# A planner for the weight slots of a two-pass decoder layer: resident w_down blocks, serpentine order, lookahead eviction

## The reference, cut to what matters

```python
h = rmsnorm(x, g_pre_mix)
p = h @ w_in                      # 1024 x 6144: xv | B | C | u | gate_conv | gate_pool
ya = (B * causal_dwconv3(C * xv)) @ w_out_conv
yb = pool_scale * groupwise_linear(trailing_mean_w(u) - u)   # w in (2, 4, 8, 16)
merged = sigmoid(gate_conv) * ya + sigmoid(gate_pool) * yb
x = x + rmsnorm(merged @ w_o, g_post_mix)
f = square(relu(rmsnorm(x, g_pre_mlp) @ w_up)) @ w_down      # 1024 x 4096, 4096 x 1024
x = x + rmsnorm(f, g_post_mlp)
```

## Time and profile before

| | |
|---|---|
| median of 3 runs | 1152.27 us (1150.86 to 1153.66) |
| the profiled execution | 1154.85 us |
| its span on the slowest core (core 0) | 1153.8 us |
| spans of the 8 cores | 1133.2 to 1153.8 us |
| mean granted TensorE clock of the cores | 0.952 to 0.961 |
| DMA traffic of core 0 | 136.50 MB |
| weight loads of the plan | 96, of which 48 from wd_bf |
| stages on core 0: w_up of pass 1, w_down of pass 1 | 322 to 431.5 us, 431.5 to 570.2 us |
| w_up of pass 2, w_down of pass 2 | 892 to 1015 us, 1015 to 1153 us |

### The profile page before, as it was taken

How to read it: one execution, slowest core, us unless ns; L and a number is a source line. 1 busy time by engine, 2 the same in 40 slices (tenths; PEclk the granted TensorE clock), 3 DMA queues, 4 the chain that set the end, 5 groups by cost and what they waited for, 6 DMA issues and landing times.

```text
span 1153.8 us, 15517 instructions; the slowest of 8 cores (1133.2 to 1153.8 us)
## 1 busy us (share of the span) xinstructions
PE 1028.5 (89%) x5289; PEld 487.0 (42%) x5289; DVE 477.2 (41%) x838; ACT 340.3 (29%) x643; POOL 173.6 (15%) x183
## 2 busy tenths in 40 slices
PE   3799689899699999888879999988976999999996
PEld 1344334344344444433335555534532555544442
DVE  4555334573533441413136655456444344412022
ACT  2322212225723333312112233322365333301011
POOL 6010002333400000000200002134043000000100
PEclk9799889899899999988979999989998999999999
DMA  9999926939353228763990743361585232136651
GB/s 213 132 135 137 131 39 81 139 33 146 60 91 74 74 74 297 242 219 112 224 167 1 111 58 53 48 100 21 114 181 104 43 74 74 74 146 237 218 201 55
DMA packets 82913, 136.50 MB, mean 118 GB/s; under 512 B 15107, under 2 KB 70467, under 8 KB 76676
## 3 DMA queue, kind: packets, MB, share of 16 engines
q0 software_dynamic: 75552, 109.58, 51.4%
q1 hardware_dynamic: 7168, 25.89, 6.7%
q10 hardware_dynamic: 116, 0.03, 0.0%
HBM read 185.11 MB, written 18.49 MB: 176 GB/s over the span
## 4 chain that ended last, share of the span: by engine, by line
PE 71%; DMA 12%; DVE 7%; issue 4%; ACT 4%; POOL 1%; DVEq 0%; ACTq 0%; SPq 0%; POOLq 0%
PE PS L121 70%; DMA WS<-w_in 4%; DMA TM<-x_p 4%; DMA WS<-w_out_conv 4%; ACT TM L138 3%; DVE TM L151 2%; DVE TM L141 2%; DVE AR L141 1%; PE PS L125 1%; DVE AR L151 1%; POOL AR L141 1%; DVE STAT L517 1%; ACT STAT L138 1%; ACT AR L138 0%; DVEq L206 0%
## 5 line engine op out<-in xcount | busy, mean ns | idle before, releaser
L121 PE MATMUL PS<-AR,WS 128*128 128x512 bf16 (+1 forms) x3520 | 682.5, 356 | 54.4 <-DVE AR L141 20.8
L121 PEld LDWEIGHTS PS<-AR,WS 128*128 128x128 bf16 x3520 | 320.3, 100 | 406.5 <-issue 91.5
L121 PE MATMUL PS<-WS,AR 128*128 128x512 bf16 x1360 | 308.4, 387 | 17.4 <-DVE TM L151 8.4
L138 ACT ACTIVATE TM<-PS 128x512 f32<-128x512 f32 (+3 forms) x270 | 158.3, 597 | 444.7 <-PE PS L121 425.9
L121 PEld LDWEIGHTS PS<-WS,AR 128*128 128x128 bf16 x1360 | 133.5, 99 | 183.1 <-issue 35.2
L141 DVE TENSOR_TENSOR AR<-TM 128x512 bf16<-128x512 f32 (+1 forms) x184 | 111.8, 622 | 164.1 <-ACT TM L138 160.8
L517 DVE RECIPROCAL STAT<-STAT 128x1 f32<-128x1 f32 x68 | 10.9, 160 | 216.6 <-ACT STAT L138 216.4
L112 POOL DMA_DIRECT2D WS<-wd_bf x48 | 25.5, 532 | 367.0 <-PE PS L121 291.6
L141 DVE TENSOR_TENSOR TM<-PS,TM 128x512 f32<-128x512 f32 (+1 forms) x56 | 35.5, 634 | 106.1 <-PE PS L121 104.3
L151 DVE SCALAR_TENSOR_TENSOR TM<-TM,CS 128x512 f32<-128x512 f32 (+1 forms) x80 | 53.7, 672 | 39.1 <-ACT TM L138 34.9
L141 POOL TENSOR_TENSOR TM<-TM 128x526 f32<-128x526 f32 (+3 forms) x36 | 42.6, 1182 | 133.1 <-ACT TM L138 69.6
(11 more groups left out here) (64 smaller groups left out, 359.4 us busy)
## 6 DMA issues: line engine op xcount, KB each, us to landing
WS<-wd_bf POOLq DMA_DIRECT2D x48, 1024.0 KB, 6.3
WS<-w_in POOLq DMA_DIRECT2D x21, 1024.0 KB, 27.2
WS<-w_up POOLq DMA_DIRECT2D x16, 1024.0 KB, 13.9
wd_bf<-w_down POOLq DMA_DIRECT2D x8, 1024.0 KB, 29.6
TM<-x_p SPq DMA_DIRECT2D x16, 512.0 KB, 6.9
y_p<-AR SPq DMA_DIRECT2D x16, 512.0 KB, 7.0
AR<-x_p SPq DMA_DIRECT2D x8, 512.0 KB, 10.9
WS<-w_out_conv POOLq DMA_DIRECT2D x4, 1024.0 KB, 14.4
```

The costliest lines, as they stand in the source:

```text
L121: return self.add("pe", lambda e: e.matmul(out, lhsT, rhs, start=start, stop=stop), reads=[lhsT, rhs], writes=[out], signal=sig, name="mm")
L138: return self.add("act", lambda e: e.activation(out, in_, func, **kw), reads=rd, writes=wr, name=name)
```

## The change

The slots are planned ahead. For each entry in order the new code looks whether its block is still in a slot; if so, nothing is loaded. If not, it takes, among the slots that its own group does not use, the one whose content is needed again latest within the entries e+1 to e+63 (not at all counts as latest), and of equals the one used longest ago. `free_after` holds the group that last used the slot. A load is issued when its own group is asked for, or earlier, at the first group g for which `free_after < g`; the loads still go out in the order of the entries. And every second token-tile group of the w_down stage runs through its eight blocks in reversed order (7 to 0), so that its first blocks are the last ones of the group before; `start` and `stop` of the accumulation follow the order. In pass 1 that is the second of three groups, in pass 2 too; the plan and the stage use the same function.

```diff
--- before.py
+++ after.py
@@ -353,6 +353,10 @@
             slot_ctr[0] += 1
             return s
 
+        def s5_order(gi_):
+            od = [(nh, kg) for nh in range(2) for kg in range(4)]
+            return od if gi_ % 2 == 0 else od[::-1]
+
         plan = []
         for ps_i in range(npass):
             nt_ = NPP // 128 + (1 if (with_sample and ps_i == npass - 1) else 0)
@@ -364,16 +368,49 @@
             plan.append([(w_o, 0, 0), (w_o, 0, 512)])
             for blk in range(DFF // 512):
                 plan.append([(w_up, 0, blk * 512)])
-            for a in range(0, nt_, 3):
-                for nh in range(2):
-                    for kg in range(4):
-                        plan.append([(w_down, kg * 1024, nh * 512)])
+            for gi_, a in enumerate(range(0, nt_, 3)):
+                for (nh, kg) in s5_order(gi_):
+                    plan.append([(w_down, kg * 1024, nh * 512)])
         entries = [e for g in plan for e in g]
         gfirst = []
+        gof = []
         acc_ = 0
-        for g in plan:
+        for gi_, g in enumerate(plan):
             gfirst.append(acc_)
             acc_ += len(g)
+            gof += [gi_] * len(g)
+        keyof = [(id(W_), r_, c_) for (W_, r_, c_) in entries]
+        slot_of, need_load, free_after = [], [], []
+        content = [None] * NSLOT
+        last_use = [-1] * NSLOT
+        for e, k_ in enumerate(keyof):
+            if k_ in content and e >= 3:
+                sl_ = content.index(k_)
+                slot_of.append(sl_)
+                need_load.append(False)
+                free_after.append(-1)
+            else:
+                same_grp = [slot_of[e2] for e2 in range(gfirst[gof[e]], e)]
+                best, best_key = None, None
+                for sl_ in range(NSLOT):
+                    if sl_ in same_grp:
+                        continue
+                    if content[sl_] is None:
+                        nu = 10 ** 9
+                    else:
+                        nu = 10 ** 9
+                        for e2 in range(e + 1, min(len(keyof), e + 64)):
+                            if keyof[e2] == content[sl_]:
+                                nu = e2
+                                break
+                    cand = (nu, -last_use[sl_])
+                    if best_key is None or cand > best_key:
+                        best, best_key = sl_, cand
+                slot_of.append(best)
+                need_load.append(True)
+                free_after.append(gof[last_use[best]] if last_use[best] >= 0 else -1)
+                content[best] = k_
+            last_use[slot_of[e]] = e
         wstate = {"g": 0, "issued": 0, "conv": 0}
         conv_ops = []
 
@@ -381,9 +418,9 @@
             def __init__(self, e, split):
                 self.split = split
                 if split:
-                    self.v = _view(WS, (e % NSLOT) * 8192, BF16, [4, KC, 128])
+                    self.v = _view(WS, slot_of[e] * 8192, BF16, [4, KC, 128])
                 else:
-                    self.v = _view(WS, (e % NSLOT) * 8192, BF16, [KC, 512])
+                    self.v = _view(WS, slot_of[e] * 8192, BF16, [KC, 512])
 
             def lhsT(self, k, jj):
                 return self.v[:, jj, k, :] if self.split else self.v[:, k, jj * 128:(jj + 1) * 128]
@@ -414,12 +451,18 @@
                     if c == 7:
                         for op_ in conv_ops:
                             op_.dma = ("wdc", P.dma_cnt["wdc"])
-            while wstate["issued"] < len(entries) and (wstate["issued"] < first + cnt or
-                                                       (wstate["issued"] - NSLOT < first and not (g == 0 and not topup))):
+            while wstate["issued"] < len(entries):
                 e = wstate["issued"]
-                assert e - NSLOT < first
+                own = e < first + cnt
+                ahead_ok = (free_after[e] < g) and not (g == 0 and not topup)
+                if not (own or ahead_ok):
+                    break
+                if own:
+                    assert free_after[e] < g
                 W, r0, c0 = entries[e]
-                if e < 3:
+                if not need_load[e]:
+                    pass
+                elif e < 3:
                     if e == 0:
                         for jj_ in range(4):
                             for e_ in range(3):
@@ -430,10 +473,10 @@
                                       deps=([xload0[min(3, len(xload0) - 1)]] if (jj_ > 0 and xload0) else []))
                 elif W is w_down:
                     src = wd_bf[(r0 // 1024) * 2 + (c0 // 512), :, :].rearrange("p (k c) -> p k c", c=512)
-                    P.dma("pool", wslot_view(e).v, src, "w%d" % (e % NSLOT), name="wload_bf", deps=conv_ops)
+                    P.dma("pool", wslot_view(e).v, src, "w%d" % slot_of[e], name="wload_bf", deps=conv_ops)
                 else:
                     src = W[r0:r0 + KC * 128, c0:c0 + 512].rearrange("(k p) c -> p k c", p=128)
-                    P.dma("pool", wslot_view(e).v, src, "w%d" % (e % NSLOT), name="wload")
+                    P.dma("pool", wslot_view(e).v, src, "w%d" % slot_of[e], name="wload")
                 wstate["issued"] += 1
             return [wslot_view(first + i) for i in range(cnt)]
 
@@ -920,17 +963,19 @@
                 bk = {}
                 for gi_, i in enumerate(G):
                     bk[i] = 2 * gi_
-                for nh in range(2):
-                    for kg in range(4):
-                        wd, = wgroup([(w_down, kg * 1024, nh * 512)])
-                        if unit_i >= 1 and pending_s0:
-                            pending_s0.pop(0)()
-                        unit_i += 1
-                        for i in G:
-                            for kk in range(KC):
-                                P.mm(PS[:, bk[i] + nh, :], actT[:, kg * 8 + kk, i * 128:(i + 1) * 128], wd.full(kk),
-                                     start=(kg == 0 and kk == 0), stop=(kg == 3 and kk == KC - 1),
-                                     signal=((kg == 3 or i == G[-1]) and kk == KC - 1))
+                od_ = s5_order(groups.index(G))
+                for (nh, kg) in od_:
+                    kgs_ = [kg2 for (nh2, kg2) in od_ if nh2 == nh]
+                    first_k, last_k = (kg == kgs_[0]), (kg == kgs_[-1])
+                    wd, = wgroup([(w_down, kg * 1024, nh * 512)])
+                    if unit_i >= 1 and pending_s0:
+                        pending_s0.pop(0)()
+                    unit_i += 1
+                    for i in G:
+                        for kk in range(KC):
+                            P.mm(PS[:, bk[i] + nh, :], actT[:, kg * 8 + kk, i * 128:(i + 1) * 128], wd.full(kk),
+                                 start=(first_k and kk == 0), stop=(last_k and kk == KC - 1),
+                                 signal=((last_k or i == G[-1]) and kk == KC - 1))
                 for i in G:
                     pm = bass.AP(PS, bk[i] * 512, [[4096, 128], [1, D]])
                     ss = stat()
```

## The result

The changed kernel takes 1370.79 us in the median (1365.16 us the fastest), against 1152.85 us before; the ratio is 1.189, with a 95% interval of 1.185 to 1.193. The prediction was 1408, range 1368 to 1450: the direction came out as written, and so did the mechanism in the main; the size was 37 us too large.

A forecast was written before the change was run, and what follows sets the result against it. TensorE, busy 89% of the span, bounds the kernel, so its standstills are paid in full. Lost prefetch, clock ramps and w_down relief sum to 255.9 us: 1154.85 + 255.9 - 2.6 = 1408 us, range 1368 to 1450.

The forecast's parts named there:

- The farthest next use belongs to the slot that was used last: Planner, pass 1: most blocks recur 48 entries later, inside the 63-entry window, so the slot just used is evicted.
- The reason given for lateness: Late groups: loads go out in order, issued only after the previous group's last matmul, so TensorE waits for issue and transfer.
- Groups 39 to 41: Pass 2, before w_up: bursts of late loads add 24.1 us each in groups 39 and 40, 17.8 in group 41.
- The length of a burst: Four loads issued together: the fourth ends near 30 us, 30.6 with 0.6 before it, at 138 GB/s.
- Groups 2 and 3: Pass 1, w_in and w_out_conv: late bursts of four loads plus two clock ramps add 7.9 and 18.4 us.
- Groups 6 to 12: Pass 1 w_up blocks: seven stalls of 8.7 us plus a 2.4 us clock ramp each add 77.7 us.
- Group 13, 35 to 38, 4 and 5: Late loads add 9.7 (13), 18.6 (35 and 36), 9.0 (37), 23.8 (38), 17.8 (4) and 11 us (5).
- w_down removed: w_down stages: 26 of 48 loads go, which TensorE does not wait for; relief of 4 us, bounds 0 and 8.
- Slower transfers because all cores ask at once: Late loads: single ones land in 10.7 instead of 8.0 us, bursts 10% later; 47 us more, 1455; chance 0.08.
- A clock that stays low inside a block: w_up blocks of pass 1 run at 1.2 GHz throughout; 80 us more, 1488; chance 0.03.
- one that does not fall: Stalls between long blocks: clock stays up, the 20 ramps cost nothing; 48 us less, 1360; chance 0.03.
- Prefetch survives: Whole kernel: repeat distance lies outside the window, oldest slot is taken, only w_down loads vanish; 1148 us; chance 0.02.

The follow-up runs named there:

- experiment 1: Changed kernel with the planner looking 23 entries ahead instead of 63: 1145.14 us, ratio 0.9954 to the kernel before.
- experiment 2: Changed kernel with the planner looking 39 entries ahead instead of 63: 1231.31 us, ratio 1.0695 to the kernel before.
- experiment 5: Kernel before with the eight w_up blocks of pass 1 sharing one slot, all else as before: 1235.94 us, ratio 1.0768.
- Experiment 4: Kernel before with the loads of w_up blocks 1 to 7 of pass 1 recorded only by their own group: 1150.28 us, ratio 1.0004.
- experiment 9: Changed kernel with the slots of two blocks of group 40 exchanged, so the u load waits for the end of group 39: 1381.81 us, ratio 1.201.
- experiment 8: Changed kernel with 40 extra matmuls, result overwritten, in front of each of w_up blocks 1 to 7 of pass 1: 1352.73 us, ratio 1.178.

## Why the prediction was right, and where it was off

**The planner.** "The farthest next use belongs to the slot that was used last" and all eight w_up blocks in one slot: right, and decided by experiments 1, 2 and 5. One number in the window turns 1.189 into 0.995; one slot for eight blocks, with nothing else of the change, costs 87 us.

**The range** held in part by luck. The bounds that the forecast adds up reach down to 1374, and nothing in it says why the range goes on to 1368; the median is 1370.79, and five of the eleven executions lie below 1368.

**The reason given for lateness** was half wrong. I read `free_after` and the issuing loop as the brake. Experiment 4 shows that in the w_up stage the loop is no brake, because POOL runs ahead of the other engines there to the first load whose slot is still being read. The list of late groups came out right because in all of them the slot's last reader was the brake too. Where it was not, I was wrong: in groups 40 and 41.

**Groups 39 to 41** are the term that was mis-sized: 66.0 predicted, 28.6 found, 37.4 of the 43.8 us between the sum (255.9) and the difference of the traces (212.1). Three things are in it.

*The early release.* The first load of group 40 takes the slot of the u block of group 39, whose last matmuls come long before the group ends. It left at 924.5, 24 us ahead, and u0 and u1 then ran beside the other three loads; the first w_o block left at 1009.6 in the same way. I had charged every load to the end of the previous group, although the order u0, u1, s2 0, ... was in front of me. By the traces of experiment 9 this is worth 4.9 us in group 40 and 4.8 in group 41, a quarter of the miss.

*The length of a burst.* I had 30.6 us from the end of a group to the use of the fourth load, from a row with 138 GB/s. In group 40 of experiment 9 it was 24.5 us (from 945.7, where the first wait began, to 970.19), with 207 GB/s, the last number here:

```profile
963.00:968.00 5.00, 5.00 (x30) 2.41 (x28) 2.58 (x6) 1.98 (x6) 1.49 (x2) 1.00 1.24 207
```

In group 39 of the changed kernel it was 27.3 us (from 864.8 to 892.06):

```profile
875.65 13.26 PE L121 MATMUL PS<-AR,WS 128*128 128x512 bf16 x64 [10.86 <-DMA WS<-w_in]
892.06 2.62 PE L121 MATMUL PS<-AR,WS 128*128 128x512 bf16 x8 [3.15 <-DMA WS<-w_out_conv]
```

That makes 6.1 and 3.3 us less than in the sum.

*The ramps and the waits that were there before.* The two ramps of 2.4 us under group 40 did not show in the time of experiment 9: the first ran beside the wait for the later loads, and at the last load the clock was at 1.00. What follows the last load there took some 4 us less than before; 2.0 of them are waits of TensorE on VectorE (9.0 us before, 6.9 in experiment 9), which the prediction had named as a bound but put at nothing. With the early release these parts make up the 20.0 us of group 40; in group 39 the burst and one ramp make up nearly all. What is left in group 41, some 6 us, I did not take apart.

**Groups 2 and 3**: 26.3 us predicted, 18.0 found. The last of the four loads landed 30.7 us after the first issue, as estimated (30), but the first issue came 1.0 us before TensorE ran out of work (121.40 and 122.39). And one clock ramp was counted twice. The timeline of TensorE at the start of group 2 (start us, us, operation, idle before):

```profile
133.43 11.39 PE L121 MATMUL PS<-AR,WS 128*128 128x512 bf16 x40 [11.04 <-DMA WS<-w_in]
146.38 1.89 PE L121 MATMUL PS<-AR,WS 128*128 128x512 bf16 x8 [1.56 <-DMA WS<-w_in]
152.18 3.41 PE L121 MATMUL PS<-AR,WS 128*128 128x512 bf16 x8 [3.91 <-DMA WS<-w_out_conv]
```

The waits are 11.0 + 1.6 + 3.9 = 16.5 us where the sum had 30.6 - 10.4 = 20.2. The 40 matmuls behind the first wait took 11.4 us instead of 8.6, so a dozen of them ran at half clock; but they run beside the wait for the later loads, and their slowness only shortens the next wait. The ramp behind the last load alone is paid. The same sum stood under groups 39 and 40.

**Groups 6 to 12**: 85.1 against 77.7. The clock term held: the seven blocks take 15.3 to 16.8 us where 13.97 is a block at full clock (experiment 8), 2.2 us more in the mean against my 2.4.

```profile
389.04 16.77 PE L121 MATMUL PS<-AR,WS 128*128 128x512 bf16 x64 [10.13 <-DMA WS<-w_up]
...
467.08 15.31 PE L121 MATMUL PS<-AR,WS 128*128 128x512 bf16 x64 [9.88 <-DMA WS<-w_up]
```

The landing did not: 8.8 to 9.4 us, 9.0 in the mean, against my 8.0, outside the 8.5 that I had as the nearer bound. Seven times 1.0 us is nearly the whole miss of 7.4. The price came from the one core whose loads landed soonest; the median of the seven others was 8.9 already.

**Group 13, 35 to 38, 4 and 5** lie within 2.2 us of their terms each.

**w_down removed**: -4 predicted, -2.2 in pass 1 and -2.4 over the rest of pass 2 (-2.6 and -0.2 in the means over the eight cores). In experiment 1, which saves nearly as many loads, they are worth about 5 us, known to 2; TensorE never waited for a w_down load itself.

**Rivals.** Slower transfers because all cores ask at once: out for the single loads, whose landings on eight cores are no longer than those of cores 1 to 7 before (median 8.9 us in both), and the bursts of four landed no later than counted. A clock that stays low inside a block, or one that does not fall: both out, by the clock rows above. The clock gate's page in the Trainium skill (TensorE: Matmul & The Clock Gate, HAM oscillation — how this bites in real kernels) has in its table that the clock stays up where a tile's compute is much longer than the wait. The w_up blocks are no test of this, since 13.8 us of matmuls are not much longer than a stall of 9.6. The end of group 38 is one: 47 us of matmuls, a stall of 10.9 us, and then 0.50, so the trace does not agree.

```profile
817.81 46.98 PE L121 MATMUL PS<-AR,WS 128*128 128x512 bf16 x280 [6.73 <-DMA WS<-w_in]
...
875.60:878.00 2.40, 2.35 (x6) 0.87 (x7) 0.00 (x0) 0.00 (x0) 0.00 (x0) 0.50 1.15 162
```

Prefetch survives: out.

## What to carry to other kernels

A slot planner that evicts what is needed farthest ahead minimises loads, not stalls: under a cyclic order of use it picks the slot that was just read, and the load then stands behind the matmul that it should hide under. Weigh how long ago a slot was last read against what the load needs (here two slots deep were enough, one was not), and keep the horizon shorter than the distance of a repeat that the slots cannot hold. To see whether a load is early, look first at which read its slot waits for, and then at what other work stands before it in the stream of the engine that issues it. And take the price of a transfer from several cores: one core's rows were 0.9 us short of the others'.

## What was not expected of the hardware

- A single converting load of 1024 KB landed in 7.8 to 8.5 us on core 0 of the kernel before and in 8.5 to 12.3 us on its seven other cores. Why core 0 was faster stays open.
- A burst of four such loads was in use 24.5, 27.3 or 29.8 us after the group before it ended (group 40 of experiment 9, groups 39 and 2 of the changed kernel). Why they differ stays open.
- 280 useless matmuls of 0.22 us made the kernel 11 us faster, because the clock stayed at 1.00 in front of six of the seven blocks. The stall of 2.7 us that the other one kept was enough for 0.50 behind it.
- POOL's queue ran through five load issues (303.3 to 307.7 us) for blocks the last of which is used some 75 us later (four blocks of 13.8 us after 327.4).
